# HGRN score levels 5 and 6 from one packed stationary operand, and four residual additions of the last tiles as products with the identity on TensorE

## The reference, cut to what matters

```python
b = jnp.cumsum(lf_i, axis=1)                       # lf_i: log of the forget gate
diff = b[:, :, None] - b[:, None, :]               # frame t against frame s
diff = jnp.where(tri[None, :, :, None, None], diff, -jnp.inf)
att = jnp.einsum('bthd,btshd->bhts', q_i, jnp.exp(diff) * k_i[:, None])
intra = jnp.einsum('bhts,bshe->bthe', att, v_i)
...
u = jnp.square(jax.nn.relu(_rms_norm(x, g_pre_ffn) @ w_up))
x = x + _rms_norm(u @ w_down, g_post_ffn)
```

## Time and profile before

| what | value |
|---|---|
| median of 3 runs | 2454.87 us (2453.24 to 2457.92) |
| the profiled execution's own time | 2455.6 us |
| its span, first to last instruction | 2453.8 us |
| mean granted TensorE clock | 0.99 |
| busy: PE / PEld / DVE / ACT / POOL | 98 / 93 / 52 / 31 / 20% |
| HGRN heads | about 690 to 1365 us |
| last product of TensorE | starts at 2428.80 us |

### The profile page before, as it was taken

How to read it: one execution, slowest core, us unless ns; L and a number is a source line. 1 busy time by engine, 2 the same in 40 slices (tenths; PEclk the granted TensorE clock), 3 DMA queues, 4 the chain that set the end, 5 groups by cost and what they waited for, 6 DMA issues and landing times.

```text
span 2453.8 us, 37235 instructions
## 1 busy us (share of the span) xinstructions
PE 2394.6 (98%) x14072; PEld 2279.7 (93%) x14072; DVE 1277.1 (52%) x2369; ACT 759.1 (31%) x1453; POOL 492.0 (20%) x729
## 2 busy tenths in 40 slices
PE   6999999999999999999999999999999999999995
PEld 6999999999999999999999999988899899899894
DVE  4052524334276667557566435455645645646638
ACT  5123232323222222222222332324232333333333
POOL 1020212102164456436445000001000000000002
PEclk8999999999999999999999999999999999999998
DMA  4252535344333324423332734223102101101113
GB/s 155 91 200 67 191 119 177 126 161 148 123 107 128 118 72 137 141 82 117 129 119 70 251 103 144 94 95 97 46 24 69 43 26 62 49 26 60 51 40 131
DMA packets 219182, 256.88 MB, mean 105 GB/s; under 512 B 8256, under 2 KB 186816, under 8 KB 218944
## 3 DMA queue, kind: packets, MB, share of 16 engines
q1 hardware_dynamic: 219072, 255.37, 31.3%
HBM read 175.12 MB, written 80.22 MB: 104 GB/s over the span
## 4 chain that ended last, share of the span: by engine, by line
PE 77%; issue 11%; DVE 5%; DMA 2%; POOL 2%; ACT 1%; SPq 1%; POOLq 0%; DVEq 0%; ACTq 0%
PE bank L607 12%; PE bank L609 12%; PE bank L608 12%; PE bank L841 5%; PE bank L843 5%; PE bank L842 5%; PE bank L892 5%; PE bank L891 5%; PE bank L890 5%; PE bank L760 3%; PE bank L869 1%; PE bank L870 1%; PE bank L871 1%; DMA ZQ<-scratch_z 1%; POOL ORS L1731 1%
## 5 line engine op out<-in xcount | busy, mean ns | idle before, releaser
L607 PE MATMUL bank<-XH,WHI 128*128 128x384 f32 x2304 | 789.1, 342 | 8.7 <-DVE XL L1292 4.3
L609 PE MATMUL bank<-XH,WLO 128*128 128x384 f32 x2304 | 773.2, 336 | 0.0
L608 PE MATMUL bank<-XL,WHI 128*128 128x384 f32 x2304 | 772.7, 335 | 0.0
L607 PEld LDWEIGHTS bank<-XH,WHI 128*128 128x128 f32 x2304 | 435.2, 189 | 15.3 <-ACT XH L933 6.2
L608 PEld LDWEIGHTS bank<-XL,WHI 128*128 128x128 f32 x2304 | 435.1, 189 | 0.8
L609 PEld LDWEIGHTS bank<-XH,WLO 128*128 128x128 f32 x2304 | 434.5, 189 | 0.0
L1262 DVE TENSOR_TENSOR WLO<-WRAW,WHI 128x1024 fp32r<-128x1024 f32 x128 | 159.7, 1248 | 255.0 <-ACT WHI L933 250.6
L933 ACT ACTIVATE ZST<-bank 128x384 f32<-128x384 f32 x240 | 117.8, 491 | 548.0 <-PE bank L609 546.2
L841 PE MATMUL bank<-XH,WHI 128*128 128x384 f32 x768 | 257.4, 335 | 3.6 <-ACT XH L933 3.6
L843 PE MATMUL bank<-XH,WLO 128*128 128x384 f32 x768 | 257.3, 335 | 0.0
L842 PE MATMUL bank<-XL,WHI 128*128 128x384 f32 x768 | 257.2, 335 | 0.0
(11 more groups left out here) (193 smaller groups left out, 3414.3 us busy)
## 6 DMA issues: line engine op xcount, KB each, us to landing
scratch_z<-ZST SPq DMA_DIRECT2D x80, 576.0 KB, 2.9
WRAW<-in_w_in SPq DMA_DIRECT2D x80, 512.0 KB, 4.0
HZ<-scratch_z SPq DMA_DIRECT2D x32, 576.0 KB, 5.1
WRAW<-in_w_up SPq DMA_DIRECT2D x32, 512.0 KB, 4.1
WDR<-in_w_down SPq DMA_DIRECT2D x32, 512.0 KB, 5.5
MG<-scratch_z SPq DMA_DIRECT2D x16, 576.0 KB, 5.7
ZQ<-scratch_z SPq DMA_DIRECT2D x4, 1152.0 KB, 6.5
ZK<-scratch_z SPq DMA_DIRECT2D x4, 1152.0 KB, 8.5
```

The lines of the kernel that those rows point to most:

```text
L607: pe.matmul(psum[c][:, 0:CH], WHI[p][:, k, :], XH[:, k, s], start=(k == 0), stop=False)
L608: pe.matmul(psum[c][:, 0:CH], WHI[p][:, k, :], XL[:, k, s], start=False, stop=False)
L609: last = pe.matmul(psum[c][:, 0:CH], WLO[p][:, k, :], XH[:, k, s], start=False, stop=(k == KT - 1))
```

## The change

Part one: KE has five slots instead of six, and the last one holds levels 5 and 6 together: for each tile the 64 key frames of level 5 (two groups of 32) and the 64 of level 6. TensorE does both levels in one product of 128 columns. In its result only three blocks mean something, and VectorE copies these to their places in ATT before the masked copies of levels 1 to 4. KE's reuse by `load_ua` becomes five slots of KE and two of UAX. Part two: tile 8 comes last in the order; the tiles with j = 2, 4, 6 and 7 are only scaled on VectorE, in ACC itself; TensorE adds identity times X1F and identity times ACC in PSUM, ScalarE copies the sum to OF after its nine squares. VectorE's order of gatherings and finishes is written anew.

```diff
+LEVK = 5
...
-        KE = [sb(f"KE{i}", [P, LEV - 1, CH], F32, ph) for i in range(2)]
-        UAX = [sb(f"UAX{i}", [P, CH], F32, ph) for i in range(2)]
+        KE = [sb(f"KE{i}", [P, LEVK, CH], F32, ph) for i in range(2)]
+        UAX = [sb(f"UAX{i}", [P, 2, CH], F32, ph) for i in range(2)]
...
-        Y_ORDER = (4, 5, 6, 7, 8, 0, 1, 2, 3)
+        Y_ORDER = (4, 5, 6, 7, 0, 1, 2, 3, 8)
+        Y_PE = (2, 4, 6, 7)
+        Y_DVE = (0, 1, 3, 5, 8)
...
-            sp.wait_ge(y_ok, j + 1)
+            if j in Y_PE:
+                sp.wait_ge(y_pk, Y_PE.index(j) + 1)
+            else:
+                sp.wait_ge(y_ok, Y_DVE.index(j) + 1)
...
-                    sp.dma_start(KE[c - 1][:, :, :], us[0:LEV - 1, :, cs].rearrange("k p t -> p k t")).then_inc(ua_in[c], 16)
-                    for k in (LEV - 1, LEV):
+                    sp.dma_start(KE[c - 1][:, :, :], us[0:LEVK, :, cs].rearrange("k p t -> p k t")).then_inc(ua_in[c], 16)
+                    for k in range(LEVK, KT):
                         sp.dma_start(UA[c][k], us[k, :, cs]).then_inc(ua_in[c], 16)
...
-                for l in range(2, LEV if t < NT - 1 else LEVS):
+                for l in range(2, LEVK if t < NT - 1 else LEVS):
                     last = pe.matmul(PSC[:, 64 + 64 * l:128 + 64 * l], KE[c % 2][:, l - 1, kt], QE[c % 2][:, l, qt],
                                      start=True, stop=True, skip_group_check=True)
+                if t < NT - 1:
+                    last = pe.matmul(PSC[:, 384:512].rearrange("p (l n) -> p l n", l=2), KE[c % 2][:, LEVK - 1, kt],
+                                     QE[c % 2][:, LEVK:LEV, qt], start=True, stop=True, skip_group_check=True)
...
+            def y_half(i, q):
+
+                return psum[2 * i + q][:, :], slice(512 * q, 512 * (q + 1))
+
+            def y_x1(i):
+
+                if i == 0:
+                    pe.wait_ge(f_r, 12 * (FF // 512))
+                pe.wait_ge(dn_ev, 31 * (FF // 512 - 1) + EV0[6] + (1, 2, 4, 6)[i])
+                pe.wait_ge(x_in[Y_PE[i]], 32)
+                for q in range(2):
+                    bank, ns = y_half(i, q)
+                    pe.matmul(bank, ident[:, :], X1F[Y_PE[i]][:, ns], start=True, stop=False, skip_group_check=True)
+
+            def y_sum(i):
+
+                pe.wait_ge(y_tt, i + 1)
+                for q in range(2):
+                    bank, ns = y_half(i, q)
+                    pe.matmul(bank, ident[:, :], ACC[:, Y_ORDER[Y_PE[i]], ns], start=False, stop=True,
+                              skip_group_check=True).then_inc(y_pe, 1)
+
+            y_x1(0)
+            for i in range(4):
+                if i < 3:
+                    y_x1(i + 1)
+                y_sum(i)
...
+            for i, j in enumerate(Y_PE):
+                if j >= 4:
+                    act.wait_ge(y_st[j % 4], 16 * (j // 4))
+                for q in range(2):
+                    act.wait_ge(y_pe, 2 * i + q + 1)
+                    last = copy(OF[j % 4][:, 512 * q:512 * (q + 1)], psum[2 * i + q][:, :])
+                last.then_inc(y_pk, 1)
...
-                for l in range(1, LEV if t < NT - 1 else LEVS):
+                if t < NT - 1:
+                    dve.tensor_copy(at[0:32, 32:64], PSC[0:32, 384:416])
+                    dve.tensor_copy(at[64:96, 96:128], PSC[32:64, 416:448])
+                    ch(dve.tensor_copy(at[0:64, 64:128], PSC[64:128, 448:512]))
+                top = LEVK if t < NT - 1 else LEVS
+                for l in range(1, top):
...
+                if j in Y_PE:
+                    dve.wait_ge(gb_in, 32)
+                    dve.scalar_tensor_tensor(ACC[:, t, :], ACC[:, t, :], yrs[:, t:t + 1], GF[:, :], ALU.mult, ALU.mult)\
+                       .then_inc(y_tt, 1)
+                    return
...
-                for p in range(4):
-                    gather(g, 6, p)
-                    y_mean(p + 1) if p < 3 else gather8(g, 6)
-                    if p < 3:
-                        finish(p)
-                for j in range(4, NT):
-                    y_mean(j)
-                    finish(j - 1)
-                finish(NT - 1)
+                gather(g, 6, 0)
+                y_mean(1)
+                finish(0)
+                gather(g, 6, 1)
+                y_mean(2)
+                gather(g, 6, 2)
+                y_mean(3)
+                finish(1)
+                gather(g, 6, 3)
+                gather8(g, 6)
+                y_mean(4)
+                for j in range(2, NT):
+                    finish(j)
+                    if j + 3 < NT:
+                        y_mean(j + 3)
...
+                    elif l >= LEVK:
+                        k56 = KE[c % 2][:, LEVK - 1, 0:n].rearrange("p (r x) -> p r x", x=P)
+                        x = lambda y: y[:, 0:n].rearrange("p (r j a w) -> p r j a w", r=n // P, a=2, w=w)[:, :, :, 0, :]
+                        dst = k56[:, :, 0:64].rearrange("p r (j w) -> p r j w", j=2) if l == LEVK else \
+                            k56[:, :, 64:P].unsqueeze(2)
+                        pool.tensor_tensor(dst, x(KK[:, s]), x(RR[:, s]), ALU.mult)
```

More of the change, by code:

```diff
@@ L165, in program @@
         UA = [[HZ[k // NC][:, k % NC * CH:(k % NC + 1) * CH] for k in range(KT - 1)] + [URAW[:, :]]] + \
-            [[KE[i][:, k, :] for k in range(LEV - 1)] + [UAX[i][:, :], HZ[2][:, (i + 1) * CH:(i + 2) * CH]] for i in range(2)]
+            [[KE[i][:, k, :] for k in range(LEVK)] + [UAX[i][:, 0, :], UAX[i][:, 1, :], HZ[2][:, (i + 1) * CH:(i + 2) * CH]] for i in range(2)]
         ph.close()
@@ L260, in program @@
         y_ss, y_ms, y_rs, y_ok = sem("y_ss"), sem("y_ms"), sem("y_rs"), sem("y_ok")
+        y_tt, y_pe, y_pk = sem("y_tt"), sem("y_pe"), sem("y_pk")
         y_st = [sem(f"y_st{i}") for i in range(4)]
@@ L1086, in piece @@
                 if i < 3 * KT:
-                    act.wait_ge(ua_in[c], 48 if c else 64)
+                    act.wait_ge(ua_in[c], 64)
                     copy(XH[:, k, cs], UA[c][k]).then_inc(sp_hi, 1)
@@ L1452, in weights @@
                                                g(MK[:, l, :]), g(src))
-                    if l < (LEV if t < NT - 1 else LEVS) - 1:
+                    if l < top - 1:
                         ch(last)
```

## The result

The changed kernel takes 2440.57 us, median of 4 runs (2439.15 to 2441.63), against 2456.39 for the kernel before beside it; the ratio is 0.9938, interval 0.9926 to 0.995. A second series gave 2443.57 against 2456.55, ratio 0.9945 (0.9931 to 0.9959). So the gain is 15.8 us, or 13.0, where 19.5 had been forecast. The sign was right and the time lies inside the range of 2432.5 to 2444.5. The size was too large: 2440.57 is just past what the bounds of the sum alone allowed (2434.3 to 2440, before the scatter). The span of the profiled execution goes from 2453.8 to 2438.3 us, 15.5 less, at a granted clock of 0.997.

A forecast was written before the change was run, and what follows sets the result against it. PE was taken to bound the heads, VectorE the last 25 us. Terms: -14.3 (part one) - 5.2 (part two) = -19.5 from the profiled 2455.6, so 2436.1, or 2435.4 us against the median; range 2432.5 to 2444.5.

The forecast's parts named there:

- What bounds each stage: PE's stream sets the time in the eight HGRN heads, VectorE's stream in the last 25 us.
- The price of the merged product: In the heads, it costs what one old product did: 0.223 us saved 64 times, 14.3 us; other bound 10.6.
- the estimate of 13.7: Saving in the heads in us, by the skill's load rule: 64 x 2 x 0.107.
- the chain behind ATT grows by 0 to 0.33: VectorE, per tile in the heads: two masked copies go, three plain copies come, 0 to 0.33 us more.
- The shorter slot takes 0.22 of that. Taken: nothing.: Heads: ATT is ready 1.1 us before PE asks in the tightest tile found, so no loss was priced.
- the copies across partitions hold up ATT: Rival in the heads: at 1.0 us a copy PE waits 37 us in all, 2472 us; 3 in 100.
- Packing gains nothing: Rival in the heads: products are paid by column, so part one gains 0, 2449.7 us; 3 in 100.
- the timetable's last gatherings: Tail, VectorE: gatherings (6,3) and tile 8's are done by 2432.0, where it was 2434.4.
- The end of VectorE: Tail: VectorE ends at 2444.9 in the old kernel's time, with a wait of 0.4 included.
- The new wait on the store of j=4: Tail: VectorE's last finish, tile 8, waits 0.4 us for that store to land and free its buffer.
- The clock stayed at its upper level: Tail; the rival said pauses let PE's clock fall to 1.2 GHz, total gain 10.5, 2444.4 us; 9 in 100.
- I take 0.7: End of tail: extra us for the last store queueing behind that of j=7, with up to 1.3 possible.

The follow-up runs named there:

- part one alone: Changed kernel with the merged product kept, but the residual additions and the order of the last tiles taken back: 2446.08 us, ratio 0.996.
- part two alone: Changed kernel with the four sums on TensorE and tile 8 last, but the HGRN heads as before: 2451.69 us, ratio 0.9981.
- contiguous: Changed kernel with levels 5 and 6 of QE side by side, so the merged product's moving operand is one piece: 2442.24 us, ratio 0.9947.
- packed_first: Changed kernel with the merged product right behind that of levels 0 and 1, ahead of the 64-column ones: 2441.84 us, ratio 0.9944.
- prep_end: `packed_first` with VectorE's preparation of the third chunk's queries moved to the end of slots 6 and 7, behind the mean: 2436.26 us, ratio 0.9917.
- no_store7: Changed kernel without the store of j=7, all arithmetic kept: 2441.85 us in a single execution, tail 19.4 us against 20.7.

## Why the prediction was right in part

**What bounds each stage** was right. In the heads, PE's stream sets the time: 10.3 us went with part one alone. In the tail, VectorE's stream and the last store do: 4.3 us with part two alone, as much as in both. The sum of separate prices was the right way to work.

**The price of the merged product** was mis-sized. The prediction had both bounds, 0.22 and 0.28, and chose: "Its excess is the shift of a start between a short and a long record and is given back by the next, so I take 14.3." The first half is right, `contiguous` against `packed_first` shows it. The second is wrong in the place where the change puts it. Ahead of it stand 64-column records, so it pays for the rise in width; behind it comes a transpose of 128 columns, so nothing gives it back. The old order had no such rise there: its ten records of 64 took 1.06, and the transpose followed them at no surcharge. Measured: 0.17 a slot, 0.05 less than assumed, in those of tiles 2 to 7; the slots of tiles 0 and 1, where no transpose follows the scores, have 0.20 and 0.25. Over the 64 slots this comes to 2.5 us. With the 2.3 at ATT that is 4.8; the first slot of head 0 and the slots of tile 8 gained some 0.6 with nothing in the change to give it, so 4.1 are missing. Why the transpose of the old order follows its 64-column records at no surcharge isn't shown. The Trainium skill, "TensorE: Matmul & The Clock Gate", section "LDWEIGHTS (loading the stationary operand)", would have given 0.214 for a saved product with its load (the estimate of 13.7). That is the price of `packed_first` (0.22 to 0.23), not of the place that the change chose.

**VectorE's chain**: "the chain behind ATT grows by 0 to 0.33" holds, with 0.13. The step that failed is the next: "The shorter slot takes 0.22 of that. Taken: nothing." It set *one* slot against a cover of 1.1 to 1.2. But from tile 2 to tile 4 VectorE works without a pause of over 0.31, so its own losses add up over these tiles, and each slot of PE comes earlier on top of the last.

VectorE's wait for PE at tile 1 might have been expected to set the two even again. It doesn't. Behind tile 1's chain stands the preparation of the second chunk's queries, and one or two of its products run beside GpSimd's SG; these end only 0.2 behind it. The timelines of GpSimd and VectorE, head 0, first before (ends 706.05 and 706.27), then after (705.14 and 705.37):

```profile
703.92 2.13 POOL L1741 TENSOR_TENSOR SG<-SG,HZ 128x384 f32<-128x384 f32 x2 [0.25 <-POOL KRH L1805]
705.09 1.18 DVE L1430 TENSOR_TENSOR PP<-PP 128x192 f32<-128x192 f32 x1
...
703.03 2.11 POOL L1802 TENSOR_TENSOR SG<-SG,HZ 128x384 f32<-128x384 f32 x2 [0.25 <-POOL KRH L1872]
704.20 1.17 DVE L1475 TENSOR_TENSOR PP<-PP 128x192 f32<-128x192 f32 x1
```

Alone such a product takes 0.35. So the chain of tile 2 starts 17.6 behind the start of the head in both kernels, though that of tile 1 starts 0.6 sooner after than before. This is read from the traces; no run moves GpSimd's work.

For head 0: from the start of the last masked copy of tile 4 to PE's next slot were 1.60 us, of which 0.37 is the least that can be (where PE does wait, it is 0.37 to 0.38). That leaves 1.23 of cover. Against the start of the head VectorE is later by 0.55: 0.38 in the chains of tiles 2, 3 and 4, the rest mostly in a pause of 0.29 ahead of the update of SH behind tile 2's chain, which wasn't there before. PE would be earlier by what slots 0 to 3 gained, 0.44 + 0.23 + 0.19 + 0.14, and 0.17 of its own, 1.17 in all. 1.72 - 1.23 = 0.49 are missing, and by 0.49 the slot is longer than a free one (-0.32 for +0.17). In heads 1, 3 and 5 VectorE loses the 0.36 to 0.38 of the three chains alone, where that copy stood 1.35 to 1.46 ahead of the next slot, and the slots lose 0.27 to 0.35. In heads 6 and 7 it stood 2.2 ahead, and they lose nothing. It decides over the whole run of tiles, and with the echo in tile 5's slot 2.3 us go in the heads. `prep_end` takes the preparation out of VectorE's way and gets all of it back: 64 slots at 0.23, the 14.3 of the prediction and a little more.

Two readings of the prediction were slightly off, and nothing hangs on them: the covers of the other tiles are 2.0 to 2.8, not 1.8 to 2.6, and the timetable's last gatherings add up to 2432.1, not 2432.0.

The rival "the copies across partitions hold up ATT" thus had the right place and the wrong price: it supposed 1.0 a copy, and one takes 0.18 to 0.23, less than the plain 128x128 copy of before. The same wait came by the accumulation instead. "Packing gains nothing" is refuted: a record of 128 columns behind another one costs 0.11, as one of 64 does. The rule of the Trainium skill quoted there (same page, section "Back-to-back issue gap"), which is for an isolated product, isn't followed by these score products.

**The tail** was right in nearly all. Last gatherings: forecast about 2432 in the old time; they start at 2419.46 and 11.22 later is 2430.68, over at 2431.96. The end of VectorE: 2444.96 against 2444.9. The new wait on the store of j=4: 0.45 against 0.4. A sum and a pair of X1 halves take 1.82 and 1.96 (2422.05 to 2423.87 to 2425.83) where 1.73 was put; it hides under VectorE's work. The clock stayed at its upper level; the Trainium skill's section "HAM oscillation — how this bites in real kernels" expects that of pauses this short, and here the trace, with 0.65 as the longest, agrees. The step that failed is "I take 0.7" for the last store: "up to 1.3 more" was its own bound, `no_store7` shows 1.3, and the 0.2 of waiting for ScalarE's copy comes on top; the landing came 1.53 later than of old. With these two stores of 512 KB, 0.38 apart, the bound was the value. Both parts thus came out at or just past the bounds that the prediction had given them (10.6 to 14.3, and 4.3 to 6.3). The sum stays inside the stated range by the two us of scatter that the prediction had allowed on top.

**The sum**: 14.3 - 4.1 + 5.2 - 0.9 = 14.5 of lasting gain; the rest of the first measurement's 15.8, and what the second one's 13.0 lacks, I put down to scatter in stretches that weren't changed. Nothing in the runs says why the start varies by three us; that stays open.

## What to carry to other kernels

If an engine works back to back over several slots, set its cover against the sum of all that these slots gain and it loses, never against one slot; and look for where it last waits for the other, and whether something third holds it behind that. Work that only later slots need goes behind everything in the slot that any other engine waits for, the small links of long chains above all. An order of products has a price of its own: put equal widths together, and price a merged product by the row of a like product with the same neighbours.

## What was not expected of the hardware

- The price of a float32 product depends on its neighbours: one of 128 columns takes 0.28 behind one of 64, and 0.22 behind another of 128; the 64-column ones behind it are 0.05 cheaper together (PE timelines of the change and of `packed_first`). In a steady stream the records of both widths are 0.11 apart.
- A copy from PSUM to other partitions showed no surcharge: 0.18 us for the 32x32 that stays on its partitions (L1493) and 0.18 for the 32x32 that moves by 32 (L1494). The 64x64 that moves takes 0.23, beside 0.29 for 128x128 in place.
- A product of VectorE that takes 0.35 alone took 1.17 beside GpSimd's SG and ended 0.2 behind it, in both kernels.
- The idle time in a wait's bracket can be much less than its cost: 0.18 in the bracket, 0.35 by the start of the product ahead, and another 0.15 in the slot behind it.
